# Sixteen more rows of the modulation weights summed on VectorE instead of multiplied on TensorE, through two ring slots

## What is computed

```python
mod_l = jnp.split((sc_lat @ w_ada[layer] + b_ada[layer])[:, None, :], 6, axis=-1)
n_lat = modulate(rmsnorm(h_lat, g_norm1[layer]), mod_l[0], mod_l[1])
mix_lat, mix_ctx = mixer_block(n_lat, n_ctx, rows, need_ctx, w_in[layer], ...)
h_lat = h_lat + mod_l[2] * mix_lat
f_lat = modulate(rmsnorm(h_lat, g_norm2[layer]), mod_l[3], mod_l[4])
h_lat = h_lat + mod_l[5] * peer_ffn(f_lat, ...)
```

## Time and profile before

| | |
|---|---|
| median of 3 runs | 2298.22 us (2297.94 to 2298.43) |
| the profiled execution | 2296.25 us, its span 2294.4 us |
| TensorE / VectorE busy | 2006.8 us (87%) / 1370.3 us (60%) |
| GpSimd / ScalarE busy | 1054.9 us (46%) / 472.5 us (21%) |
| granted TensorE clock, mean | 0.983 of full |
| chain that ended last | TensorE 45%, DMA 36%, GpSimd 11% |
| moved by DMA | 787.26 MB, 343 GB/s on the mean |

### The profile page before, as it was taken

The page is one execution under the profiler, slowest core; times in us unless marked ns, Lnnn a source line. Parts: engine busy times, 40 slices in busy tenths (PEclk is TensorE's granted clock), DMA queues, the critical chain, the costliest instruction groups (busy, mean ns, idle before and its releaser), DMA issues.

```text
span 2294.4 us, 21913 instructions
## 1 busy us (share of the span) xinstructions
PE 2006.8 (87%) x8122; PEld 1160.3 (51%) x8122; DVE 1370.3 (60%) x2153; ACT 472.5 (21%) x1019; POOL 1054.9 (46%) x929
## 2 busy tenths in 40 slices
PE   6999999999999999899988998978877777777776
PEld 4443348888888888764543544423322222222222
DVE  5645964788873544865555456556556655665644
ACT  3116740344331000111101110111111011111011
POOL 0012323899991100255454445655555555555542
PEclk9999999999999999989999999999999999999999
DMA  9977885445558989899999999999999999999996
GB/s 338 332 231 193 312 308 178 135 144 147 146 147 299 379 315 325 315 397 409 414 417 414 417 421 421 422 422 421 422 422 421 421 422 421 422 422 421 421 421 269
DMA packets 253694, 787.26 MB, mean 343 GB/s; under 512 B 25578, under 2 KB 171186, under 8 KB 178450
## 3 DMA queue, kind: packets, MB, share of 16 engines
q0 software_dynamic: 83792, 574.96, 61.5%
q1 hardware_dynamic: 158116, 201.45, 26.6%
q10 hardware_dynamic: 11680, 9.44, 1.3%
HBM read 772.12 MB, written 9.47 MB: 341 GB/s over the span
## 4 chain that ended last, share of the span: by engine, by line
PE 45%; DMA 36%; POOL 11%; issue 3%; DVE 3%; ACT 1%; ACTq 0%; DVEq 0%; POOLq 0%
DMA vb<-in_peer_v,eidx 34%; PE ps L2376 13%; PE ps L1339 9%; PE ps L2297 4%; PE ps L2239 4%; PE ps L1546 3%; PE ps L1309 3%; PE ps L1324 2%; PE ps L1575 1%; PE ps L1284 1%; POOL vb L1751 1%; POOL big L593 1%; POOL big L565 1%; POOL big L562 1%; POOL big L563 1%
## 5 line engine op out<-in xcount | busy, mean ns | idle before, releaser
L2376 PE MATMUL ps<-vb,diag 128*128 128x512 f32 x2048 | 950.7, 612 | 228.8 <-DMA vb<-in_peer_v,eidx 226.5
L2376 PEld LDWEIGHTS ps<-vb,diag 128*128 128x128 f32 x2048 | 380.8, 193 | 787.0 <-issue 408.2
L1751 POOL DMA_INDIRECT vb<-in_peer_v,eidx x256 | 409.0, 1598 | 521.1 <-PE ps L2376 502.6
L2160 DVE CUSTOM_DVE_ANT_0 nT<-nT,f 128x2048 f32<-128x2048 f32 x167 | 382.0, 2291 | 321.4 <-DMA nT<-in_peer_u,eidx 321.0
L1339 PE MATMUL ps<-nT,w_ring 128*128 128x256 f32 (+1 forms) x1472 | 381.6, 417 | 0.0
L1339 PEld LDWEIGHTS ps<-nT,w_ring 128*128 128x128 f32 x1472 | 276.2, 190 | 95.6 <-issue 65.9
L2160 DVE CUSTOM_DVE_ANT_0 mT<-mT,f 128x2048 f32<-128x2048 f32 x84 | 192.3, 2291 | 161.9 <-DMA mT<-in_peer_u,eidx 161.7
L1751 POOL DMA_INDIRECT nT<-in_peer_u,eidx x167 | 183.7, 1100 | 68.0 <-issue 49.7
L1924 ACT ACTIVATE gel<-hd 128x2 f32<-128x2 f32 (+1 forms) x130 | 26.1, 202 | 891.5 <-DVE hd L2160 891.4
L1904 ACT ACTIVATE diag<-ident,wgt 128x128 f32<-128x128 f32 x256 | 90.8, 394 | 100.8 <-PE ps L2376 86.9
L1751 POOL DMA_INDIRECT mT<-in_peer_u,eidx x84 | 93.0, 1108 | 32.2 <-issue 25.0
(11 more groups left out here) (416 smaller groups left out, 2181.4 us busy)
## 6 DMA issues: line engine op xcount, KB each, us to landing
w_ring<-in_w_ada SPq DMA_DIRECT2D x80, 1024.0 KB, 7.1
w_ring<-in_w_in SPq DMA_DIRECT2D x50, 1024.0 KB, 7.9
w_ring<-in_w_ada POOLq DMA_DIRECT2D x16, 1024.0 KB, 5.6
w_ring<-in_peer_w_query SPq DMA_DIRECT2D x16, 1024.0 KB, 27.6
w_ring<-in_w_proj_b SPq DMA_DIRECT2D x8, 1024.0 KB, 9.6
w_ring<-in_w_proj_a SPq DMA_DIRECT2D x8, 1024.0 KB, 9.7
w_ring<-in_w_out SPq DMA_DIRECT2D x8, 1024.0 KB, 9.4
vb<-in_w_out SPq DMA_DIRECT2D x5, 1024.0 KB, 12.9
```

What stands on the lines that cost most here:

```text
L1751: pool.indirect_dma_start(row, None, table, bass.IndirectOffsetOnAxis(ap=eidx[:, i % 3, j:j + 1], axis=0))\
L2160: v.tensor_tensor_reduce(u_buffer(m), u_buffer(m), f[:, i // HEADS], 1.0, 0.0, ALU.mult, ALU.add, hd[:, i % 2, m % K:m % K + 1]).then_inc( ...
L2376: last = pe.matmul(ps[:, 4 * tile + c, :], diag[:, m % NDIAG], vb[m % NV][:, c * 512:(c + 1) * 512], start=(r == 0), stop=(r == HEADS * K ...
```

## The change

The 16 units of block 2 leave TensorE and SyncE's plan. `row_vector` and `load_row` now take 32 rows, n = 0 to 15 of block 2 and 16 to 31 of block 3, in the slots 3 and 4 in turn, so that a load waits for the row before last. Block 2 sums into `kzero`'s tile, widened to 128 partitions, and a new tile `first_b`; `last_rows(0)` sums them over the partitions into bank 6 after the third pair of gate columns. VectorE takes four rows ahead of `conv(0)`, one after each of `conv(0..3)`, four more, one between `q_of(k)` and `scans(k)`, and two after each of the gates 0 to 5. `input_weights` moves from the gates 2 and 3 to 4 and 5, `late_rows(0)` from before gate 0 to after gate 6. GpSimd issues 14 row loads ahead of the bias and B loads, one after each U column's stores (which now also wait for the stores before), and ten behind the gathers, ahead of `store_mods(0)`. The pairs of the gate columns use three slots; slots 3 and 4 go back to the ring after the rows 30 and 31.

```diff
-LATE_PER_PAIR = {3: (1, 0), 4: (3, 1), 5: (3, 1), 6: (3, 1), 7: (2, 1)}
+ROWS_FIRST, ROWS_AFTER_CONV, ROWS_PER_GATE = 4, 4, 2
...
-        n_late = [0]
-
-        def plan_late(count):
-            for _ in range(count):
-                ada_at.append(plan_ada(*late[n_late[0]], 3))
-                n_late[0] += 1
-
-        row_free = freed_by[4]
-        freed_by[4] = (last_used, KD)
-        plan_first(NB // 2, turn[NB % 3])
-        plan_second(NB // 2, turn[(NB + 1) % 3])
-        for n, (before, after) in LATE_PER_PAIR.items():
-            plan_first(n + 1, turn[(2 * n + 2) % 3])
-            plan_late(before)
-            plan_second(n + 1, turn[(2 * n + 3) % 3])
-            plan_late(after)
-        last_wide = n + 1
-        n_slot = [turn[(2 * last_wide + 2) % 3]]
+        row_free = freed_by[3:5]
+        for x in range(2):
+            freed_by[3 + x] = (last_used, 2 * KD - 1 + x)
+        first_stage = len(pairs) - NSTAGE
+        for n in range(NB // 2, first_stage):
+            plan_first(n, turn[2 * n % 3])
+            plan_second(n, turn[(2 * n + 1) % 3])
+        n_slot = [turn[2 * first_stage % 3]]
...
-        last_at = [None] * KD
+        last_at = [None] * (2 * KD)
 
         def plan_last():
-            c, k = late[n_late[0] + len(last_at)]
+            c, k = late[len(last_at)]
...
-        kzero = sb("kzero", [H, G, H])
+        kz_all = sb("kzero", [P, G * H])
+        kzero = kz_all[0:H].rearrange("p (g h) -> p g h", g=G)
+        first_b = sb("first_b", [P, D - G * H])
...
+        first_sums = [(kz_all, 0, G * H), (first_b, G * H, D)]
...
+        row_landed, row_base = [row_in, s5_in], [0, 16 * 9]
...
-            def load_row(k):
-
-                if k == 0:
-                    pool.wait_ge(row_free[0], row_free[1])
+            def load_row(n):
+
+                if n < 2:
+                    pool.wait_ge(row_free[n][0], row_free[n][1])
                 else:
-                    pool.wait_ge(last_used, k)
-                at = LATE_CHUNKS[1] * D
-                pool.dma_start(row_view(w_ring[:, 4]), t["w_ada"][0, k * P:(k + 1) * P, at:at + D])\
-                    .then_inc(row_in, 16)
-
-            load_row(0)
+                    pool.wait_ge(last_used, n - 1)
+                q, k = divmod(n, KD)
+                at = LATE_CHUNKS[q] * D
+                pool.dma_start(row_view(w_ring[:, 3 + n % 2]), t["w_ada"][0, k * P:(k + 1) * P, at:at + D])\
+                    .then_inc(row_landed[n % 2], 16)
+
+            LRU_ROW = ROWS_FIRST + 4 + ROWS_AFTER_CONV
+            for n in range(LRU_ROW + 2):
+                load_row(n)
...
-            load_row(1)
             for k in range(KW):
-                if 2 * k + 2 < KD:
-                    load_row(2 * k + 2)
                 pool.wait_ge(acc_free, U0 + k + 1)
+                if k >= 1:
+                    pool.wait_ge(u_out, 128 * k)
                 for b in range(8):
                     at = (b % GS) * NC
                     dst = u_dram[:, :, 2 * k + b // GS, at:at + NC].rearrange("s h c -> h s c")
                     pool.dma_start(dst, zu[b * H:(b + 1) * H, k % 2]).then_inc(u_out, 16)
-                if 2 * k + 3 < KD:
-                    load_row(2 * k + 3)
+                load_row(LRU_ROW + 2 + k)
             pool.wait_ge(u_out, 128 * KW)
             for r in range(4):
...
+            for n in range(LRU_ROW + 2 + KW, 2 * KD):
+                load_row(n)
             store_mods(0)
...
-            def row_vector(k):
-
-                v.wait_ge(row_in, 16 * (k + 1))
-                w = row_view(w_ring[:, 4])
-                for n, (total, lo, hi) in enumerate(sums):
+            def row_vector(n):
+
+                q, k = divmod(n, KD)
+                v.wait_ge(row_landed[n % 2], row_base[n % 2] + 16 * (n // 2 + 1))
+                w = row_view(w_ring[:, 3 + n % 2])
+                for x, (total, lo, hi) in enumerate((first_sums, sums)[q]):
                     if k == 0:
                         ins = tsc(total, w[:, lo:hi], scol[:, k, 0:1], None, ALU.mult)
                     else:
                         ins = stt(total, w[:, lo:hi], scol[:, k, 0:1], total, ALU.mult, ALU.add)
-                    if n < len(sums) - 1:
+                    if x == 0:
                         step(ins)
                     else:
                         ins.then_inc(last_used, 1)
-                        v.wait_ge(last_used, k + 1)
-
+                        v.wait_ge(last_used, n + 1)
+
+            for n in range(ROWS_FIRST):
+                row_vector(n)
             for k in range(4):
                 conv(k)
-            row_vector(0)
+                row_vector(ROWS_FIRST + k)
+            n_row = ROWS_FIRST + 4
+            for n in range(ROWS_AFTER_CONV):
+                row_vector(n_row + n)
+            n_row += ROWS_AFTER_CONV
             for k in range(KW):
                 q_of(k)
-                row_vector(2 * k + 1)
+                row_vector(n_row)
+                n_row += 1
                 scans(k)
-                if k < KW - 1:
-                    row_vector(2 * k + 2)
                 if k + 4 < KW:
                     conv(k + 4)
...
                 v.wait_ge(mods_out, 32 * q + 16)
-                if q == 0:
-                    v.wait_ge(ada_used, KD * (NFIRST + 1))
-                else:
-                    v.wait_ge(last_sum, q)
+                v.wait_ge(last_sum, q + 1)
                 tt(mod_rows[:], ps[:, (6, 7, 0)[q], :], mod_rows[:], ALU.add).then_inc(mod_free, 1)
 
-            late_rows(0)
...
-                if k in (2, 3):
-                    input_weights(k - 2)
+                for _ in range(min(ROWS_PER_GATE, 2 * KD - n_row)):
+                    row_vector(n_row)
+                    n_row += 1
+                if k in (4, 5):
+                    input_weights(k - 4)
+                if k == KW - 2:
+                    late_rows(0)
...
-            def ada_unit(bank):
-
-                k = ada_n[0] % KD
-                w = row_view(unit(pe, ada_at[ada_n[0]]))
-                ada_n[0] += 1
-                for j in range(4):
-                    last = pe.matmul(ps[32 * j:32 * j + 32, bank, :], scol[:, k, :], w[:, j * 512:(j + 1) * 512],
-                                     start=(k == 0), stop=(k == KD - 1))
-                last.then_inc(ada_used, 1)
-
-            def late_unit():
-
-                if ada_n[0] == NFIRST * KD:
-                    pe.wait_ge(acc_free, V0 + 5)
-                ada_unit(6)
...
-                pe.wait_ge(last_used, KD * q)
+                pe.wait_ge(last_used, KD * (q + 1))
                 if q == 2:
                     pe.wait_ge(acc_free, L0 + KW)
                 for j in range(4):
                     at = slice(j * 512, (j + 1) * 512)
-                    for total, lo, hi in (sums if q == 1 else [(fin_sum, 0, D)]):
+                    for total, lo, hi in (first_sums, sums, [(fin_sum, 0, D)])[q]:
                         a, b = max(lo, at.start), min(hi, at.stop)
                         if a < b:
-                            last = pe.matmul(ps[32 * j:32 * j + 32, (7, 0)[q - 1], a - at.start:b - at.start],
+                            last = pe.matmul(ps[32 * j:32 * j + 32, (6, 7, 0)[q], a - at.start:b - at.start],
...
-                    columns_by_halves(V0 + 2 * c, 0, 2 * T, [(n, j) for n in range(2) for j in range(2)])
+                    columns_by_halves(V0 + 2 * c, 0, 2 * T)
                     break
-                spots = ((), ()) if c < KW // 2 else ((7, 15), (7, 15))
-                for j, _ in enumerate(columns(V0 + 2 * c, 0, 2 * T, spots)):
+                for j, _ in enumerate(columns(V0 + 2 * c, 0, 2 * T)):
...
+                if c == KW // 2 - 2:
+                    last_rows(0)
```

23 lines of the change are left out of this document (8 added, 15 removed).

## The result

| | before | after |
|---|---|---|
| median | 2298.08 us (2295.7 to 2298.43, 4 runs) | 2321.77 us (2320.6 to 2324.99, 4 runs) |
| ratio to before | | 1.0098 (95% interval 1.0086 to 1.011) |
| the profiled execution, its span | 2296.25 us, 2294.4 us | 2322.41 us, 2320.6 us |
| TensorE / VectorE busy | 2006.8 / 1370.3 us | 1995.0 / 1419.9 us |
| granted TensorE clock, mean | 0.983 | 0.977 |

What follows compares the result with a forecast made beforehand. TensorE bounds most of the kernel, but GpSimd ends the S5 stages. GpSimd's S5 work starts 36.2 us late, 23.6 of it slack; the remaining 12.6 us raise the executed 2296.3 to 2308.9, the median to 2311, range 2297 to 2325.

Steps and rivals of the forecast that it cites:

- Part 1 (rows leave TensorE): Before the gate columns: 16 rows at 1.0 us each leave TensorE, 16.0 us less; a new summing product adds about 1.0.
- T: Start of TensorE's gate columns, 335.81 us before the change; forecast to move by -7.8 us, to 328.0.
- Part 2 (start-up): First convolutions and gates: rows delay VectorE, and TensorE waits +4.1 us at both first and second gates, +8.2 together.
- Part 3 (rows in the gate columns): Gate columns: two rows take 9.2 us, not 6.9, so VectorE's input weights are ready at T +70.8 us, 398.8.
- the landing: Time for a row's load to land in the gate columns: 9 us for row 22, 6.3 for later ones.
- ring waits: Gate columns: with three ring slots instead of five TensorE waits for w_in loads, 10 us, under VectorE's 398.8.
- Part 4 (GpSimd's start): GpSimd's S5 work waits for the store of vector 2 and begins at 405.2 instead of 368.97, 36.2 us late.
- Part 4 (the slack): S5 stages: GpSimd's idle 23.17 + 0.44 us absorb 23.6 us of its lateness; 12.6 us pass to the end.
- (a): Rival for the gate-column loads: they keep up, no change, 2294 to 2302, say 2298; chance 0.20.
- (b): Rival: faster, loads keep up and the start-up wait is under 5 us too, -7, 2291; chance 0.10.
- (c): Rival for the S5 stages: GpSimd makes up its lateness at 18.2 us a stage, 2306; chance 0.10.
- The Trainium skill's rule on a DMA's length: Row loads: 2.0 us plus bytes at 436 GB/s, 4.4 us each; the sum would be 2301.

Runs made afterwards that it cites:

- c_one: Changed kernel with its 16 VectorE rows placed elsewhere, one ahead of the first convolution and one in each of eight gate columns; 2301.79 us, ratio 1.0011.
- e_no_row_loads: Changed kernel without the loads of rows 22 to 31, VectorE still adding up what lies in the slots; 2306.36 us, ratio 1.0028.
- b_late_23: Old kernel with GpSimd's S5 work held back until the last gate column was copied; 2308.09 us, ratio 1.0036.
- b_late_30: Old kernel with GpSimd's S5 work held back until the row sum of vector 3; 2312.02 us, ratio 1.0053.
- e_weights_early: Changed kernel with the two halves of the input weights back behind gates 2 and 3; 2320.59 us, ratio 1.0086.
- e_conv_first: Changed kernel with no row ahead of the first convolution and eight instead of four behind the convolutions; 2317.55 us, ratio 1.0073.
- c_one_3: As c_one, but three rows after the convolutions instead of five and four before gate 0 instead of two; 2318.99 us, ratio 1.008.
- e_both_early: As e_weights_early, with vector 2's sum, bias addition and store also moved ahead; 2315.86 us, ratio 1.0065.
- c_one_gath: As c_one, but the u gathers issued behind row 27's load; 2302.37 us, ratio 1.0008.
- c_one_early: As c_one_gath, but three rows instead of two in each of recurrences 4 to 7, and one only in gates 0 to 3; 2305.36 us, ratio 1.0019.
- experiments 1 and 2: Old kernel with GpSimd's S5 work held back, 2308.09 and 2312.02 us; the first again without four of VectorE's five M products from the fourth stage, 2297.41 us.

## Why the prediction was right, point by point

The forecast was 2311 us, in a range of 2297 to 2325; measured were 2321.8. The sign, the place and the order of the mechanism held, and the range with them. The 10.8 us between came from two terms of the sum.

- **Part 1 (rows leave TensorE).** Held. T moved from 335.8 to 326.3 us. With the start-up of 8.4 (below) the rows gave back 17.9 us instead of 16.0, 1.12 us each.
- **Part 2 (start-up).** The sum held, in part by luck. Row 0 was used at 157.22 and row 1 at 160.77 (forecast 158.7 and 160.5); the convolutions began at 171.47 (171.3). The first U column started at 203.71 instead of 195.34, +8.4 against +8.2. Its make-up was another: the waits were 4.97 and 1.10 us instead of 4.1 and 4.1, and 2.8 us from the lower clock, of which nothing was said, happened to fill what the second wait lacked. These are the rows that answer to the earlier trace rows:

```profile
157.22 0.75 DVE L1089 TENSOR_SCALAR kzero<-w_ring,scol 128x1024 f32<-128x1024 f32 x1 [4.42 <-DMA w_ring<-in_w_ada]
160.77 1.28 DVE L1091 SCALAR_TENSOR_TENSOR kzero<-w_ring,scol,kzero 128x1024 f32<-128x1024 f32 x1 [2.01 <-DMA w_ring<-in_w_ada]
...
337.42 0.63 DVE L1190 TENSOR_TENSOR gst<-mT,gst 128x256 f32<-128x256 f32 x1 [8.51 <-ACT gst L814]
351.96 0.95 DVE L1091 SCALAR_TENSOR_TENSOR last_c<-w_ring,scol,last_c 128x704 f32<-128x704 f32 x1 [7.31 <-DMA w_ring<-in_w_ada]
...
362.60 0.95 DVE L1091 SCALAR_TENSOR_TENSOR last_c<-w_ring,scol,last_c 128x704 f32<-128x704 f32 x1 [3.98 <-DMA w_ring<-in_w_ada]
```

- **Part 3 (rows in the gate columns).** The mechanism held, a term was small. VectorE waited 7.31 us for row 22 and 3.98 for row 24. From the issue of row 24's load (354.86) to that of row 30's (384.18) three turns of two rows took 9.8 us each instead of 9.2, and `bb_ready` came at T + 74.7 instead of T + 70.8. What was mis-sized is the landing. On VectorE's chain row 22 took 10.5 us to land instead of 9.0, and rows 24, 26 and 28 took 7.65, 5.16 and 7.52, 6.8 on the mean instead of 6.3; row 29 was waited for too, 0.83 us. The ten row loads of this stretch spread from 5.0 to 11.0 us around a median of 7.6 (DMA issues from 340 to 395 us, KB each and us to landing):

```profile
w_ring<-in_w_ada POOLq DMA_DIRECT2D x10, 1024.0 KB, 7.6
w_ring<-in_w_in SPq DMA_DIRECT2D x6, 1024.0 KB, 9.2
```

  The ring waits (0.89, 4.15, 0.77) were 5.8 us, under the 10 that the forecast took, and hidden behind VectorE, as it said.
- **Part 4 (GpSimd's start).** The chain from `bb_ready` to the first product took 7.1 us (6.4 forecast). The start was 2.9 us later than forecast: -1.7 from T, +3.9 from the rows, +0.7 here.
- **Part 4 (the slack).** This is the term that failed: "23.6 of that are slack". Start of the first product and of the 16th PB (the PB columns from the one profiled execution, the time from the medians):

| kernel | first product | 16th PB | time against before |
|---|---|---|---|
| before | 368.97 | 671.85 | |
| `c_one` | 385.09 | 673.54 | +1.8 |
| `e_no_row_loads` | 391.23 | 677.78 | +6.2 |
| `b_late_23` | 391.36 | 677.82 | +8.2 |
| `b_late_30` | 398.87 | 685.85 | +12.1 |
| `e_weights_early` | 406.27 | 693.84 | +20.7 |
| after | 408.13 | 694.33 | +23.7 |

  In the last five rows, where GpSimd waits for nothing behind its first product, the 16th PB follows that product by 286.2 to 287.6 us, so it reaches 671.85 with a start near 385.4: the slack is some 16.5 us. (It is 284.1 us in `e_conv_first`, and 288.5 to 296.7 in `c_one`, `c_one_3`, `e_both_early`, `c_one_gath` and `c_one_early`, whose second PB had to wait for TensorE, 1.36 us in the first and 16.75 us in the last.) Of the 7.1 us that were missing, 3.1 are the first pass (18.5 us instead of 15.4) and 3.4 the fourteen stages behind the second PB (267.7 us from 426.59 to 694.33, 264.4 before). The 264.4 also hold the idle 0.44 us that the forecast counted as slack and that is gone after, so these stages grew by 3.8; together that is 6.9 of the 7.1. Both are GpSimd beside VectorE (experiments 1 and 2); over the last 13 stages its instructions took 231.9 us in all instead of 228.6. I had read 15.4 us from a stretch in which VectorE did something else, and added it to a start at which it wouldn't. So 39.2 - 16.5 = 22.7 us pass through, and the 16th PB is 22.5 us late. The forecast had 12.6.
- **The rest.** 2.9 + 7.1 is 10.0 of the 10.8 us; the other 0.8 I can't place. It is less than the spread of the four times (2320.6 to 2324.99).
- **The rivals.** (a) and (b) needed every term at its lower bound, 5.1 us for each landing among them; on the chain one row did that (5.16), row 22 took 10.5 and two others 7.5 and 7.65. (c) was wrong in the same way as the forecast's slack, and more so: GpSimd's stage didn't fall to 18.2 us, it rose. It does fall to 18.0 when VectorE leaves out its products.
- **The Trainium skill's rule on a DMA's length** (DMA: Bandwidth & Descriptors, Anatomy of one DMA) would have given 2301, an estimate. With 7.6 us as the median landing in the stretch that counts, where the DMA engines were full, the trace goes further from its 4.4 us than before.
